# Strassen products over all row tiles, with 24 weight sums made early in the kernel

## The chip, the cores and the metric

The kernel runs on one core of one Trainium2 chip. The metric is the device time of one execution in microseconds (us), the median of several runs. One further execution was profiled; its trace is what is read below.

## What is computed

One layer of a hybrid decoder trunk, in float32, for 1024 tokens of width 2048. `h = RMSNorm(x)`; one input projection `proj = h @ w_in` gives queries, keys, values and gates of three head groups: dilated window attention (A), forgetting attention (B) and chunked gated linear attention (C, also GLA). Their outputs times SiLU(gate) are concatenated, projected and added to x:

```python
    proj = jnp.einsum('bsd,de->bse', h, w_in)
    ...
    mixed = jnp.concatenate([
        out_a.astype(h.dtype) * jax.nn.silu(az),
        out_b.astype(h.dtype) * jax.nn.silu(bz),
        out_c.astype(h.dtype) * jax.nn.silu(cz)], axis=-1)
    return x + jnp.einsum('bse,ed->bsd', mixed, w_out)
```

The change touches the last matrix product, `mixed @ w_out` (1024 x 2048 by 2048 x 2048), and work beside the first.

## The kernel before

Every float32 product is made of three rounded matmuls: an operand is split into a high and a low part (ScalarE rounds the high one, `hi`; VectorE subtracts, `lo`), and hi x hi, hi x lo and lo x hi are added up in PSUM. Each engine has its own program, written out in `build`; they meet at semaphores. SyncE (SP) only issues DMAs, in program order: where it waits, all that is queued behind it waits.

**Input projection.** It runs in column groups of 128 columns. A group has four quarters of the contraction (`kq`), each with one load of 256 KB into one of two buffers of `w_raw` (`load_quarter`), one rounding, one subtraction and 24 matmuls of 512 tokens (`half_quarter`). `load_quarter` waits until the quarter two places back is split. Groups 2 to 7 of the `C_ALONE` = 8 first groups have nothing else beside them; on SP they are a hardware loop of 24 loads (line 713). Behind that loop on SP stand the store `gate_stack <- gate_split` (line 767), then in `gla_loads(0)` the loads `rank_rows`, `gate_up`, `gate_bias` (734 to 736), which wait for that store to land, and only then the weights of group 8. GpSimd (POOL) makes `level_mask` (lines 1086 to 1105) when `gate_stack` has landed, and VectorE waits for it (`levels_ready`, line 1850) in front of group 8's second quarter.

**Attention.** One pair of heads after another, each beside four column groups. In the last pair (`LAST` = 9) there are no more input columns; TensorE then makes the first 512 output columns from 15 of the 16 row tiles of `mixed` (`early_quarter`), in three rounds, stored to `partial`. A row tile is 128 of the 2048 rows of the contraction. VectorE's order there is written in `last_body`: per slot the attention steps, the first weight split, the late steps, the other splits. Line 2045 is `scale`, the last step of a softmax; its result is turned by TensorE (line 2489).

**Output projection.** `out_quarter` makes columns 512 to 1023 from 16 row tiles into the 8 PSUM banks, one per 128 tokens. Then comes the Strassen part: columns 1024 to 2047 for 14 of the row tiles. Tokens, row tiles and columns are each cut into halves, which gives 2 x 2 blocks on each side and 7 products instead of 8. A product needs a sum or difference of two weight quarters (`FAST_WEIGHTS`) and of two row quarters (`FAST_ROW_SUMS`), both made by GpSimd (lines 1205 and 1217), and is then added by VectorE to one or two output blocks (`FAST_INTO`, `merge`, line 2222). A run of `FAST_RUNS` is a product (7 items, one per row tile, each 4 banks x 3 matmuls) or a "left" run: row tiles 8 and 9 for both column groups, and row tile 9 for columns 0 to 511, over all 8 banks:

```python
FAST_RUNS = [("product", 0), ("product", 1), ("left", 0), ("left", 1), ("left", 2)] + [("product", q) for q in range(2, 7)]
```

An item's weights go through one of four slots: two loads (`load_terms`), the sum on GpSimd (`weight_sum`), the split (`terms_hi`, `terms_lo`), three items ahead of TensorE (`fast_item`). At a run's first item TensorE waits until its banks' earlier tiles are merged (`out_summed`).

Of the kernel before, what the change touches and what calls it, by code (L numbers as in the profile page):

```python
# [4 lines left out]
P = 128  # L5
# [164 lines left out]
def weight_loads(n):  # L170

    r, j = run_of(n)
    kind, q = FAST_RUNS[r]
    if kind == "left":
        return [(LEFT_ROWS[q][j], LEFT_COLS[q])]
    one, op, two = FAST_WEIGHTS[q]
    return [(FAST_ROWS[kh][j], FAST_CGS[nh] * HALF) for kh, nh in ((one, two) if op is not None else (one,))]


def weight_op(n):  # L180

# [212 lines left out]
def build(nc, x, norm_g, w_in, a_q_gain, a_k_gain, b_q_gain, b_k_gain, fox_bias,  # L394
# [6 lines left out]
    mixed = nc.dram_tensor("mixed_scratch", (D_MODEL, SEQ), F32, kind="Internal").ap()  # L401
    partial = nc.dram_tensor("partial_scratch", (SEQ, HALF), F32, kind="Internal").ap()
# [3 lines left out]
    with ExitStack() as ctx:  # L406
# [60 lines left out]
        c_sum = sb("c_sum", [B_HEADS, SEQ], scope=first)  # L467
        gate_raw, gate_split = x_tile[0:GATE_ROWS, 0, 0:GATE_COLS], x_tile[0:GATE_ROWS, 1, 0:GATE_COLS]
# [83 lines left out]
        merged_into = [fast_out[0], fast_out[1], res]  # L552
# [96 lines left out]
        def _(sp):  # L649
# [312 lines left out]
            def load_fast_residual(c, t):  # L962
                cols = slice(FAST_CGS[c] * HALF, (FAST_CGS[c] + 1) * HALF)
                sp.dma_start(fast_out[c][:, t, :], x_rows[t * P:(t + 1) * P, cols]).then_inc(x_in[c], 16)

            def load_partial(t):
                sp.wait_ge(out_saved[t], 32)
                sp.dma_start(res[:, t, :], partial[t * P:(t + 1) * P, :]).then_inc(res_in[t], 16)

            def load_rows_again(th, kh, j):  # L970

                k = FAST_ROWS[kh][j]
                sp.wait_ge(quarter_done, 3 * (GROUPS + AHEAD) + EARLY - len(ROUNDS) + OUT_ORDER.index(k) + 1)
                sp.dma_start(raw_rows(th, kh, j), mixed[k * P:(k + 1) * P, th * HALF:(th + 1) * HALF])\
                    .then_inc(mix_in[0 if th == kh else 1 + kh], 16)

            def load_terms(n):
# [6 lines left out]
                for to, (k, col) in zip((t_ones[slot], t_twos[slot]), weight_loads(n)):  # L984
                    sp.dma_start(to, w_out_k[:, k, col:col + HALF]).then_inc(terms_in[slot], 16)
# [14 lines left out]
            for kk in range(3, 6):  # L1000
                load_out_quarter(1, kk)
            sp.wait_ge(mix_lo, MIX_ALL)
            load_res(1)
            for kk in range(6, KT):
# [5 lines left out]
                elif kk <= 11:  # L1010
# [3 lines left out]
                    else:  # L1014
                        for t in range(2 * (kk - 8), 2 * (kk - 8) + 2):
                            load_fast_residual(1, t)
                else:
                    load_rows_again(1, 1, kk - 12)
                    for t in range(2 * (kk - 12), 2 * (kk - 12) + 2):
                        load_fast_residual(0, t)  # L1020
            load_terms(2)
            load_rows_again(1, 1, 4)
            load_terms(3)
            load_rows_again(1, 1, 5)
            load_terms(4)
            load_terms(5)
            load_rows_again(1, 1, 6)
            load_terms(6)
            load_terms(7)
            for n in range(8, FAST_ITEMS):  # L1030
# [4 lines left out]
                if 8 <= n < 8 + FAST_K:  # L1035
                    load_rows_again(1, 0, n - 8)
                if 14 <= n < 18:
                    for t in range(2 * (n - 14), 2 * (n - 14) + 2):
                        load_partial(t)
                if 18 <= n < 18 + FAST_K:  # L1040
                    load_rows_again(0, 1, n - 18)
                if 28 <= n < 32:
                    for t in range(2 * (n - 28), 2 * (n - 28) + 2):
                        save_merged(2, t)
                if 45 <= n < 49:
                    save_merged(0, 4 + n - 45)
# [11 lines left out]
        def _(pool):  # L1058
# [20 lines left out]
            pool.memset(gate_raw, 0.0).then_inc(zeroed, 1)  # L1079

# [1573 lines left out]
```

## Time and profile before

| what | value |
|---|---|
| three runs | 2038.71 to 2040.92 us, median 2040.43 |
| the profiled execution | 2044.43 us |
| its span, first to last instruction | 2042.7 us, mean granted clock 0.998 |
| TensorE busy | 2008.2 us, 98% |
| VectorE busy | 1121.9 us, 55% |
| ScalarE busy | 891.1 us, 44% |
| GpSimd busy | 503.1 us, 25% |
| DMA | 223.20 MB, mean 109 GB/s |

Busy is time with an instruction under way; the rest is idle. A matmul of 512 columns is shown as 0.39 us long, but the next starts before it ends, so the pace is read from starts or from counts per stretch. An idle time is put down to the event that ended it. Idle time of an engine that is not the limit costs nothing by itself.

### The profile page before, as it was taken

Reading aid. Unit: us, or ns where it says so; the run is one execution under the profiler, and the core shown is the slowest. Engines: PE = TensorE matmul, PEld = TensorE weight load, DVE = VectorE, ACT = ScalarE, POOL = GpSimd, SP = SyncE. Lnnn points to the kernel's source line nnn. Section 1 sums busy time; section 2 is a strip of 40 time slices with the busy share of each in tenths; the row PEclk is TensorE's granted clock in tenths of the full one; section 3 lists DMA queues with packets and bytes.
Section 4 is the critical chain, followed back from the end, with each engine's and each line's share of the span. In section 5 each row is a group of like instructions: output and inputs, shape, how many; then the busy total and the mean of one; then the engine's idle time right before and its main releaser. Section 6 shows DMA issues by size and latency. Waiting matters only on the chain.

```text
span 2042.7 us, 28729 instructions
## 1 busy us (share of the span) xinstructions
PE 2008.2 (98%) x10024; PEld 1690.6 (83%) x10024; DVE 1121.9 (55%) x1733; ACT 891.1 (44%) x1504; POOL 503.1 (25%) x400
## 2 busy tenths in 40 slices
PE   6999999999999999999999999999999999999998
PEld 5788888888888888888888888888888887788787
DVE  7611456465445555555555555555555657613797
ACT  7311343444454445445454445445444556411242
POOL 0000343251531212222221212222122210002565
PEclk9999999999999999999999999999999999999999
DMA  7322424324332222222222222323232274466646
GB/s 236 81 72 71 116 68 109 100 82 103 94 98 78 61 85 78 87 67 72 87 72 85 64 89 79 107 58 98 83 97 71 85 249 145 134 200 222 237 155 196
DMA packets 204559, 223.20 MB, mean 109 GB/s; under 512 B 17336, under 2 KB 143336, under 8 KB 203328
## 3 DMA queue, kind: packets, MB, share of 16 engines
q1 hardware_dynamic: 187760, 191.73, 31.8%
q10 hardware_dynamic: 16720, 30.45, 4.0%
q8 instruction: 46, 0.75, 0.2%
q14 instruction: 33, 0.27, 0.0%
HBM read 173.35 MB, written 48.78 MB: 109 GB/s over the span
## 4 chain that ended last, share of the span: by engine, by line
PE 85%; DVE 7%; ACT 2%; DMA 2%; issue 2%; POOL 1%; SPq 0%; DVEq 0%; ACTq 0%; POOLq 0%
PE acc L2266 19%; PE acc L2268 19%; PE acc L2267 19%; PE pv L2504 4%; PE turned L2489 4%; PE scores L2481 2%; PE scores L2478 2%; DVE w_lo L1724 1%; DVE act_lo L2209 1%; DMA w_raw<-in_w_in_dram 1%; PE acc L2616 1%; DVE fast_out L2222 1%; PE acc L2553 1%; PE acc L2555 1%; PE acc L2554 1%
## 5 line engine op out<-in xcount | busy, mean ns | idle before, releaser
L2266 PE MATMUL acc<-act_hi,w_hi 128*128 128x512 f32 x1848 | 737.1, 399 | 2.5 <-DVE w_lo L1724 1.9
L2268 PE MATMUL acc<-act_hi,w_lo 128*128 128x512 f32 x1848 | 722.0, 391 | 0.0
L2267 PE MATMUL acc<-act_lo,w_hi 128*128 128x512 f32 x1848 | 720.7, 390 | 0.0
L2268 PEld LDWEIGHTS acc<-act_hi,w_lo 128*128 128x128 f32 x1848 | 346.9, 188 | 75.4
L2266 PEld LDWEIGHTS acc<-act_hi,w_hi 128*128 128x128 f32 x1848 | 347.5, 188 | 69.5 <-DVE w_lo L1724 4.8
L2267 PEld LDWEIGHTS acc<-act_lo,w_hi 128*128 128x128 f32 x1848 | 347.7, 188 | 65.2
L1724 DVE TENSOR_TENSOR w_lo<-w_raw,w_hi 128x512 fp32r<-128x512 f32 x223 | 199.4, 894 | 358.6 <-ACT w_hi L1239 358.3
L1545 ACT ACTIVATE prob<-prob,neg_max 128x128 f32<-128x128 f32 (+7 forms) x160 | 124.0, 775 | 251.1 <-DVE neg_max L2035 251.1
L1159 POOL TENSOR_TENSOR vz<-raw 32x512 f32<-32x512 f32 x72 | 85.6, 1189 | 468.3 <-ACT sq L1492 465.6
L1239 ACT ACTIVATE w_hi<-w_raw 128x512 fp32r<-128x512 f32 x223 | 139.1, 624 | 137.2 <-PE acc L2268 110.1
L2051 DVE TENSOR_TENSOR pt_lo<-turned,pt_hi 128x1024 fp32r<-128x1024 f32 (+1 forms) x120 | 114.9, 957 | 146.9 <-ACT pt_hi L1553 146.3
L1553 ACT ACTIVATE pt_hi<-turned 128x1024 fp32r<-128x1024 f32 (+1 forms) x120 | 97.6, 814 | 201.3 <-PE turned L2489 201.0
L1173 POOL TENSOR_TENSOR q_st<-raw,q_st 64x512 fp32r<-64x512 f32 x40 | 58.8, 1469 | 355.3 <-ACT q_st L1519 353.8
L2035 DVE CUSTOM_DVE_ANT_0 prob<-scores,logit_bias 128x128 f32<-128x128 f32 (+7 forms) x160 | 117.9, 753 | 40.3 <-PE scores L2481 39.6
L1282 ACT ACTIVATE stage<-acc 128x512 f32<-128x512 f32 x112 | 66.9, 597 | 113.0 <-PE acc L2268 112.7
L2489 PE MATMUL turned<-ident,prob 128*128 128x128 f32 x720 | 98.5, 273 | 1.9 <-DVE prob L2045 1.7
L2489 PEld LDWEIGHTS turned<-ident,prob 128*128 128x128 f32 x720 | 84.4, 141 | 13.0 <-issue 3.3
L2504 PE MATMUL pv<-pt_lo,v_st 128*128 128x256 f32 (+1 forms) x400 | 94.9, 292 | 0.0
L2504 PE MATMUL pv<-pt_hi,v_st 128*128 128x256 f32 (+1 forms) x400 | 88.3, 270 | 2.8 <-DVE pt_lo L2051 2.8
L2045 DVE TENSOR_SCALAR prob<-prob,inv_denom 128x128 f32<-128x128 f32 (+7 forms) x160 | 83.2, 520 | 5.7
L2504 PEld LDWEIGHTS pv<-pt_hi,v_st 128*128 128x128 f32 x400 | 75.9, 190 | 11.8 <-issue 3.5
L2481 PE MATMUL scores<-k_lo,q_st 128*128 128x128 f32 (+2 forms) x240 | 83.7, 353 | 0.0
(427 smaller groups left out, 3007.0 us busy)
## 6 DMA issues: line engine op xcount, KB each, us to landing
w_raw<-in_w_in_dram SPq DMA_DIRECT2D x240, 256.0 KB, 2.9
proj_scratch<-stage ACTq DMA_DIRECT2D x116, 256.0 KB, 2.1
w_raw<-in_w_out_dram SPq DMA_DIRECT2D x64, 256.0 KB, 3.5
raw<-proj_scratch SPq DMA_DIRECT2D x20, 512.0 KB, 3.4
logit_bias<-in_w_out_dram SPq DMA_DIRECT2D x35, 256.0 KB, 4.6
act_lo<-mixed_scratch SPq DMA_DIRECT2D x7, 1024.0 KB, 8.6
t_raw<-in_w_out_dram SPq DMA_DIRECT2D x28, 256.0 KB, 3.7
extra_raw<-in_w_out_dram SPq DMA_DIRECT2D x23, 256.0 KB, 3.5
```

Of the source, the lines that this page charges most:

```text
L1239: act.activation(w_hi[:, slot, :], w_raw[:, slot, :], ACT.Copy).then_inc(hi_done, 1)
L1545: act.activation(prob[:, j % 2, 0:n], prob[:, j % 2, 0:n], ACT.Exp, scale=-1.0, bias=neg_max[:, j:j + 1], accum_out=denom[:, j:j + 1]).the ...
L1553: act.activation(pt_hi[:, 0:n], turned[:, 0:n], ACT.Copy).then_inc(pth_done, 1)
L1724: dve.tensor_tensor(w_lo[:, slot, :], w_raw[:, slot, :], w_hi[:, slot, :].bitcast(F32), ALU.subtract)\
L2035: dve.tensor_tensor_reduce(out=prob[:, j % 2, 0:n], in0=scores[:, c0:c0 + n], in1=bias, scale=1.0, scalar=3e38, op0=ALU.add, op1=ALU.min, ...
L2051: dve.tensor_tensor(pt_lo[:, 0:n], turned[:, 0:n], pt_hi[:, 0:n].bitcast(F32), ALU.subtract)\
L2266: pe.matmul(acc, hi, xh, start=first, stop=False)
L2267: pe.matmul(acc, hi, xl, start=False, stop=False)
L2268: mm = pe.matmul(acc, lo, xh, start=False, stop=end)
L2481: mm = pe.matmul(scores[:, o + c0:o + c1], q, k_lo[:, h, c0:c1], start=False, stop=True)
L2489: mm = pe.transpose(turned[:, o:o + P], prob[:, q, c * P:(c + 1) * P], ident[:])
L2504: mm = pe.matmul(pv[:, (2 * (d % 2) + q) * P:(2 * (d % 2) + 2) * P], v_st[:, h, c, :], (pt_hi, pt_lo)[part][:, o:o + (2 - q) * P], start=( ...
```

## The change

- The Strassen part covers all 16 row tiles: 8 row tiles in each half, and row tile 9 stands last in the second half. Of the left runs only the one for columns 0 to 511 stays (one item), and it runs first. The products are renumbered.
- Products 2 and 6 (`FAST_ON_TOP`) start on the banks of products 0 and 4 without clearing them, so an output block gets the sum in one merge; product 0 and 4 then go into one block only.
- For products 1, 2 and 4 the 24 weight sums are made in groups 2 to 7 of the input projection: SP loads two weight quarters into `g_wide`, GpSimd adds them, SP stores the sum to `summed` in DRAM. In the Strassen part such an item has one load and no sum.
- Row tiles 8 and 9 of `mixed` are also stored to DRAM, since their halves are loaded again for row sums. The merges' targets and the loads of x and of `partial` into them trade places; a product's merges are spread over 6 items.
- In slot 28 of the last pair VectorE's late steps (the last `scale`) stand ahead of the slot's first split.

```diff
+LATE_FIRST = 28
...
 FAST_CGS = (2, 3)
-FAST_ROWS = (list(range(7)), [7] + list(range(LAST + 1, KT)))
-FAST_LEFT = (LAST - 1, LAST)
+FAST_ROWS = (list(range(LAST - 1)), [LAST - 1] + list(range(LAST + 1, KT)) + [LAST])
 FAST_K = len(FAST_ROWS[0])
-FAST_WEIGHTS = (((0, 1), ALU.subtract, (1, 1)), ((1, 0), ALU.subtract, (0, 0)), ((0, 0), ALU.add, (1, 1)),
-                ((0, 0), None, None), ((1, 1), None, None), ((0, 0), ALU.add, (0, 1)), ((1, 0), ALU.add, (1, 1)))
-FAST_ROW_SUMS = (None, None, ((0, 0), ALU.add, (1, 1)), ((1, 0), ALU.add, (1, 1)), ((0, 0), ALU.add, (0, 1)),
-                 ((1, 0), ALU.subtract, (0, 0)), ((0, 1), ALU.subtract, (1, 1)))
-FAST_INTO = (((1, 0, ALU.add), (1, 1, ALU.add)), ((0, 1, ALU.add), (0, 0, ALU.add)),
-             ((0, 0, ALU.add), (1, 1, ALU.add)), ((0, 1, ALU.add), (1, 1, ALU.subtract)),
-             ((1, 0, ALU.add), (0, 0, ALU.subtract)), ((1, 1, ALU.add),), ((0, 0, ALU.add),))
-FAST_RUNS = [("product", 0), ("product", 1), ("left", 0), ("left", 1), ("left", 2)] + [("product", q) for q in range(2, 7)]
-LEFT_ROWS = (FAST_LEFT, FAST_LEFT, FAST_LEFT[1:])
-LEFT_COLS = (FAST_CGS[0] * HALF, FAST_CGS[1] * HALF, 0)
+FAST_WEIGHTS = (((0, 1), ALU.subtract, (1, 1)), ((1, 0), ALU.subtract, (0, 0)), ((0, 0), ALU.add, (0, 1)),
+                ((0, 0), None, None), ((0, 0), ALU.add, (1, 1)), ((1, 1), None, None), ((1, 0), ALU.add, (1, 1)))
+FAST_ROW_SUMS = (None, None, ((1, 0), ALU.subtract, (0, 0)), ((1, 0), ALU.add, (1, 1)), ((0, 0), ALU.add, (1, 1)),
+                 ((0, 0), ALU.add, (0, 1)), ((0, 1), ALU.subtract, (1, 1)))
+FAST_ON_TOP = (2, 6)
+SUMMED_SOONER = (1, 2, 4)
+SOONER = [(q, j) for q in SUMMED_SOONER for j in range(FAST_K)]
+SOONER_AT = 0
+FAST_INTO = (((1, 0, ALU.add),), ((0, 1, ALU.add), (0, 0, ALU.add)), ((1, 1, ALU.add),),
+             ((0, 1, ALU.add), (1, 1, ALU.subtract)), ((1, 1, ALU.add),), ((1, 0, ALU.add), (0, 0, ALU.subtract)),
+             ((0, 0, ALU.add),))
+FAST_RUNS = [("left", 2)] + [("product", q) for q in range(7)]
+LEFT_ROWS = {2: (LAST,)}
+LEFT_COLS = {2: 0}
 RUN_SIZE = [FAST_K if kind == "product" else len(LEFT_ROWS[q]) for kind, q in FAST_RUNS]
 RUN_FIRST = [sum(RUN_SIZE[:r]) for r in range(len(FAST_RUNS))]
 RUN_LAST = [f + n - 1 for f, n in zip(RUN_FIRST, RUN_SIZE)]
 FAST_ITEMS = sum(RUN_SIZE)
 FAST_SLOTS = 4
+MERGE_STEPS = 6
 SPLIT_BEFORE = Q_OUT + EARLY + KT
 USED_BEFORE = 3 * (GROUPS + AHEAD) + EARLY - len(ROUNDS) + KT - 1
 FAST_SUMS = (len(FAST_INTO) - 2) * FAST_K
-ROW_SUM_STEP = [first + j for first in (9, 16, 23, 30, 37) for j in range(FAST_K)]
+ROW_SUM_STEP = [first + j for first in (4, 12, 20, 28, 36) for j in range(FAST_K)]
...
+    return weight_terms(q, j)[:1 if q in SUMMED_SOONER else 2]
+
+
+def weight_terms(q, j):
...
-            out += own[2 * (n - e - 1):2 * (n - e)]
+            out += [own[i] for i in range(len(own)) if e + 1 + i * MERGE_STEPS // len(own) == n]
...
+        sooner = [[g_wide[:, (2 * i + e) * HALF:(2 * i + e + 1) * HALF] for e in range(2)] for i in range(2)]
...
-            with sp.Fori(AHEAD, C_ALONE) as s:
-                for kq in range(4):
-                    load_quarter(s, kq, COL_CQ + s * P)
+            def load_sooner(i):
+
+                if i == 0:
+                    sp.wait_ge(x_turned, 4 * NT)
+                elif i >= 2:
+                    sp.wait_ge(small_saved, 16 * i)
+                for to, (k, col) in zip(sooner[i % 2], weight_terms(*SOONER[i])):
+                    sp.dma_start(to, w_out_k[:, k, col:col + HALF]).then_inc(row_summed, 16)
+
+            def store_sooner(i):
+                sp.wait_ge(t_summed, i + 1)
+                sp.dma_start(summed[i * P:(i + 1) * P, :], sooner[i % 2][0]).then_inc(small_saved, 16)
+
+            for n in range(4 * (C_ALONE - AHEAD)):
+                load_quarter(AHEAD + n // 4, n % 4, COL_CQ + (AHEAD + n // 4) * P)
+                if 0 <= n - SOONER_AT - 1 < len(SOONER):
+                    store_sooner(n - SOONER_AT - 1)
+                if 0 <= n - SOONER_AT < len(SOONER):
+                    load_sooner(n - SOONER_AT)
+            for i in range(4 * (C_ALONE - AHEAD) - SOONER_AT - 1, len(SOONER)):
+                store_sooner(i)
+            sp.wait_ge(small_saved, 16 * (len(SOONER) + 1))
...
+                if n == 7:
+                    store_pair(LAST - 1)
                 if n == 10:
                     sp.wait_ge(mix_lo, mixed_by(KK_GATED, 1))
+                    sp.wait_ge(mixed_saved, 16 * LAST)
...
+                kind, q = FAST_RUNS[run_of(n)[0]]
+                if kind == "product" and q in SUMMED_SOONER:
+                    i = SOONER.index((q, run_of(n)[1]))
+                    sp.dma_start(t_ones[slot], summed[i * P:(i + 1) * P, :]).then_inc(terms_in[slot], 16)
+                else:
+                    for to, (k, col) in zip((t_ones[slot], t_twos[slot]), weight_loads(n)):
+                        sp.dma_start(to, w_out_k[:, k, col:col + HALF]).then_inc(terms_in[slot], 16)
...
+            sp.wait_ge(o_done, LAST + 3)
+            sp.dma_start(mixed[LAST * P:(LAST + 1) * P, :], vz[:]).then_inc(mixed_saved, 16)
             sp.wait_ge(mix_lo, MIX_ALL)
+            sp.wait_ge(mixed_saved, 16 * PAIRS)
...
+            for i, (q, _j) in enumerate(SOONER):
+                pool.wait_ge(row_summed, 32 * (i + 1))
+                pool.tensor_tensor(sooner[i % 2][0], sooner[i % 2][0], sooner[i % 2][1], FAST_WEIGHTS[q][1]).then_inc(t_summed, 1)
...
                     steps(slot)
+                    if slot == LATE_FIRST:
+                        late(slot)
                     for n in early_at(slot)[:1]:
                         split_next(n + EARLY_AHEAD)
-                    late(slot)
+                    if slot != LATE_FIRST:
+                        late(slot)
                     for n in early_at(slot)[1:]:
...
+                on_top = kind == "product" and q in FAST_ON_TOP
...
-                    pe.matmul(banks[b], hi, t_his[slot], start=first, stop=False)
-                    pe.matmul(banks[b], hi, t_los[slot], start=False, stop=False)
-                    mm = pe.matmul(banks[b], lo, t_his[slot], start=False, stop=at_end)
+                    pe.matmul(banks[b], hi, t_his[slot], start=first and not on_top, stop=False,
+                              skip_group_check=on_top)
+                    pe.matmul(banks[b], hi, t_los[slot], start=False, stop=False, skip_group_check=on_top)
+                    mm = pe.matmul(banks[b], lo, t_his[slot], start=False, stop=at_end, skip_group_check=on_top)
```

SP's queue in the input projection. Before, each pass of the loop of line 713 issues four loads, and this stands behind it:

```order
L656 ISA [waits lo_done]
L656 DMA w_raw<-in_w_in_dram 128x4x128
L713 COMPARE_AND_BRANCH
L767 DMA gate_scratch<-x_tile 80x1408 [waits gate_lows]
L734 DMA rank_rows<-gate_scratch 80x1024 [waits gate_saved,c_saved,c_done]
L735 DMA gate_up<-gate_scratch 80x96
L736 DMA gate_bias<-in_gla_gate_bias_dram 96x1
L656 DMA w_raw<-in_w_in_dram 128x4x128 [waits lo_done] x2
```

Now the loop is written out; these are its last pass and what follows (`t_summed` is GpSimd's sum, `small_saved` counts landed stores):

```order
L668 DMA w_raw<-in_w_in_dram 128x4x128 [waits lo_done]
L736 DMA summed_scratch<-g_wide 128x512 [waits t_summed]
L732 DMA g_wide<-in_w_out_dram 128x512 [waits small_saved]
L732 DMA g_wide<-in_w_out_dram 128x512
L736 DMA summed_scratch<-g_wide 128x512 [waits t_summed]
L798 DMA gate_scratch<-x_tile 80x1408 [waits gate_lows,small_saved]
```

Between two weight loads of the input projection there are now a wait for a sum, a store and two loads, and `gate_scratch` stands behind the last sum and the landing of its store.

GpSimd's queue from `iota` to the masks, now:

```order
L1127 IOTA dist_i 128x1024 [waits consts]
L1131 MEMSET x_tile 80x1408 [waits x_turned]
L1135 TENSOR_TENSOR g_wide<-g_wide 128x512 [waits row_summed] x24
L1142 MEMSET level_mask 128x896 [waits gate_lows,c_saved,gate_saved,small_saved,c_done]
L1143 MEMSET ident_both 128x256
```

The 24 sums of line 1135 are new; the other rows stood in the same order without them.

VectorE's queue at the last scale of the last pair, before:

```order
L2035 ISA neg_max 128x1
L2155 TENSOR_TENSOR act_lo<-w_raw,act_hi 128x512
L2043 RECIPROCAL inv_denom<-denom 128x1
L2045 TENSOR_SCALAR prob<-prob,inv_denom 128x1024
L2155 TENSOR_TENSOR w_lo<-extra_raw,w_hi 128x512
```

and now:

```order
L2094 ISA neg_max 128x1
L2102 RECIPROCAL inv_denom<-denom 128x1
L2104 TENSOR_SCALAR prob<-prob,inv_denom 128x1024
L2217 TENSOR_TENSOR act_lo<-w_raw,act_hi 128x512
L2217 TENSOR_TENSOR w_lo<-extra_raw,w_hi 128x512
```

The reciprocal and the scale have moved ahead of one weight split.

## Rows read from the trace of the kernel before

**Rows 1.** The page: busy engines, and the chain that ended last.
```profile
PE 2008.2 (98%) x10024; PEld 1690.6 (83%) x10024; DVE 1121.9 (55%) x1733; ACT 891.1 (44%) x1504; POOL 503.1 (25%) x400
...
PE 85%; DVE 7%; ACT 2%; DMA 2%; issue 2%; POOL 1%; SPq 0%; DVEq 0%; ACTq 0%; POOLq 0%
```
**Rows 2.** Windows: stretch, length, busy us (and instructions) of each engine, clock, DMA share, GB/s.
```profile
1850.00:1900.00 50.00, 50.00 (x221) 41.16 (x220) 19.31 (x28) 9.89 (x16) 14.87 (x12) 1.00 0.78 265
80.00:220.00 140.00, 139.66 (x616) 115.31 (x616) 25.22 (x33) 29.14 (x44) 7.79 (x21) 1.00 0.32 86
1950.00:2000.00 50.00, 50.00 (x220) 40.97 (x219) 49.52 (x53) 22.09 (x38) 36.71 (x24) 1.00 0.49 164
```
**Rows 3.** Timeline (start, length) and waits (us, times, longest) in the Strassen part.
```profile
1921.78 0.39 PE L2618 MATMUL side<-w_hi,act_lo 128*128 128x512 f32 x1
1923.03 0.47 PE L2616 MATMUL acc<-t_hi,act_hi 128*128 128x512 f32 x1 [0.86 <-DVE fast_out L2222]
...
2037.09 0.69 DVE L2222 TENSOR_TENSOR fast_out<-fast_out,scores 128x512 f32<-128x512 f32 x1
...
PE acc L2616 <- DVE fast_out L2222: 1.7, 2, 0.9
PE acc L2616 <- DVE w_lo L2201: 0.3, 1, 0.3
```
**Rows 4.** Timeline at the last scale of the last pair.
```profile
1771.82 0.39 PE L2555 MATMUL acc<-act_hi,act_lo 128*128 128x512 f32 x1
1773.66 0.52 PE L2489 MATMUL turned<-ident,prob 128*128 128x128 f32 x3 [1.46 <-DVE prob L2045]
...
1771.23 0.18 ACT L1545 ACTIVATION_READ_ACCUMULATOR prob<-prob,neg_max 128x1 f32 x1
...
1772.77 0.75 DVE L2045 TENSOR_SCALAR prob<-prob,inv_denom 128x1024 f32<-128x1024 f32 x1
```
**Rows 5.** Timeline of SyncE's queue, at the loop's first load and behind the loop.
```profile
88.78 0.39 SPq L656 DMA_DIRECT2D w_raw<-in_w_in_dram  x1
...
208.10 0.36 SPq L767 DMA_DIRECT2D gate_scratch<-x_tile  x1
212.00 0.34 SPq L734 DMA_DIRECT2D rank_rows<-gate_scratch  x1
...
213.33 3.79 SPq L656 DMA_DIRECT2D w_raw<-in_w_in_dram  x2
```
**Rows 6.** Timeline of GpSimd behind the loop; in brackets the idle time before.
```profile
212.06 0.85 POOL L1086 MEMSET level_mask<- 128x896 f32 x1 [152.50 <-DMA gate_scratch<-x_tile]
...
218.62 4.80 POOL L1105 TENSOR_SCALAR_AFFINE_SELECT level_mask<-level_mask 128x64 f32<-128x64 f32 x14
```
**Rows 7.** Timeline of ScalarE where TensorE ends group 7.
```profile
226.22 0.60 ACT L1282 ACTIVATE stage<-acc 128x512 f32<-128x512 f32 x1 [2.04 <-PE acc L2268]
```
**Rows 8.** Landings (KB, us) of late loads: alone at 1944.98, followed at 1919.49, four at 1825.
```profile
logit_bias<-in_w_out_dram SPq DMA_DIRECT2D x1, 256.0 KB, 3.3
...
1948.39 1.45 POOL L1205 TENSOR_TENSOR t_raw<-t_raw,logit_bias 128x512 f32<-128x512 f32 x1 [1.45 <-DMA logit_bias<-in_w_out_dram]
...
logit_bias<-in_w_out_dram SPq DMA_DIRECT2D x1, 256.0 KB, 3.8
...
fast_out<-in_x_dram SPq DMA_DIRECT2D x2, 256.0 KB, 4.4
```
**Rows 9.** Landings in the stretch 80 to 220 us.
```profile
w_raw<-in_w_in_dram SPq DMA_DIRECT2D x29, 256.0 KB, 2.9
proj_scratch<-stage ACTq DMA_DIRECT2D x12, 256.0 KB, 2.1
```
**Rows 10.** GpSimd's weight sums and row sums: ns least/median/most, first and last start.
```profile
L1205 POOL TENSOR_TENSOR t_raw<-t_raw,logit_bias x20: 1285/1296/1835, 1812.2 to 2026.5; 128x512 f32<-128x512 f32 x20
...
L1217 POOL TENSOR_TENSOR row_sum<-act_lo,act_hi x21: 1281/1687/1837, 1919.8 to 2011.8; 128x512 f32<-128x512 f32 x21
```
**Rows 11.** Windows of TensorE alone, behind a wait of 2.8 us that ended at 1688.79.
```profile
1688.00:1692.00 4.00, 3.21 (x14) 0.57 0.81 229
```

More of the change, by code:

```diff
@@ L182, in weight_op @@
     kind, q = FAST_RUNS[run_of(n)[0]]
-    return FAST_WEIGHTS[q][1] if kind == "product" else None
+    return FAST_WEIGHTS[q][1] if kind == "product" and q not in SUMMED_SOONER else None
 def weights_landed(n):
@@ L401, in build @@
     mixed = nc.dram_tensor("mixed_scratch", (D_MODEL, SEQ), F32, kind="Internal").ap()
+    summed = nc.dram_tensor("summed_scratch", (len(SOONER) * P, HALF), F32, kind="Internal").ap()
     partial = nc.dram_tensor("partial_scratch", (SEQ, HALF), F32, kind="Internal").ap()
@@ L983, in load_terms @@
                     sp.wait_ge(lo_done, SPLIT_BEFORE - 3 + n)
-                for to, (k, col) in zip((t_ones[slot], t_twos[slot]), weight_loads(n)):
-                    sp.dma_start(to, w_out_k[:, k, col:col + HALF]).then_inc(terms_in[slot], 16)
+                kind, q = FAST_RUNS[run_of(n)[0]]
+                if kind == "product" and q in SUMMED_SOONER:
+                    i = SOONER.index((q, run_of(n)[1]))
+                    sp.dma_start(t_ones[slot], summed[i * P:(i + 1) * P, :]).then_inc(terms_in[slot], 16)
+                else:
+                    for to, (k, col) in zip((t_ones[slot], t_twos[slot]), weight_loads(n)):
+                        sp.dma_start(to, w_out_k[:, k, col:col + HALF]).then_inc(terms_in[slot], 16)
             def save_merged(c, t):
@@ L1015, in _ @@
                         for t in range(2 * (kk - 8), 2 * (kk - 8) + 2):
-                            load_fast_residual(1, t)
+                            load_fast_residual(t)
                 else:
-                    load_rows_again(1, 1, kk - 12)
+                    if kk == 12:
+                        load_rows_again(0, 0, FAST_K - 1)
+                    load_rows_again(1, 0, kk - 12)
                     for t in range(2 * (kk - 12), 2 * (kk - 12) + 2):
-                        load_fast_residual(0, t)
+                        load_partial(t)
             load_terms(2)
-            load_rows_again(1, 1, 4)
+            load_rows_again(1, 0, 4)
             load_terms(3)
-            load_rows_again(1, 1, 5)
+            load_rows_again(1, 0, 5)
             load_terms(4)
             load_terms(5)
-            load_rows_again(1, 1, 6)
+            load_rows_again(1, 0, 6)
             load_terms(6)
             load_terms(7)
+            load_rows_again(1, 0, 7)
             for n in range(8, FAST_ITEMS):
@@ L1035, in _ @@
                 if 8 <= n < 8 + FAST_K:
-                    load_rows_again(1, 0, n - 8)
+                    load_rows_again(1, 1, n - 8)
                 if 14 <= n < 18:
                     for t in range(2 * (n - 14), 2 * (n - 14) + 2):
-                        load_partial(t)
+                        load_first_residual(t)
                 if 18 <= n < 18 + FAST_K:
                     load_rows_again(0, 1, n - 18)
-                if 28 <= n < 32:
-                    for t in range(2 * (n - 28), 2 * (n - 28) + 2):
+                if 20 <= n < 24:
+                    for t in range(2 * (n - 20), 2 * (n - 20) + 2):
                         save_merged(2, t)
-                if 45 <= n < 49:
-                    save_merged(0, 4 + n - 45)
+                if 48 <= n < 52:
+                    save_merged(0, 4 + n - 48)
             for t in range(4):
@@ L1211, in sum_rows @@
                 if u == 0:
-                    pool.wait_ge(mix_in[0], mix_landed(0) + 16 * 2 * FAST_K)
-                elif j == 0 and q in (3, 4):
-                    pool.wait_ge(mix_in[q - 2], mix_landed(q - 2) + 16 * FAST_K)
+                    pool.wait_ge(mix_in[0], mix_landed(0) + 16 * FAST_K)
+                    pool.wait_ge(mix_in[1], mix_landed(1) + 16 * FAST_K)
+                elif j == 0 and q == 3:
+                    pool.wait_ge(mix_in[2], mix_landed(2) + 16 * FAST_K)
+                elif j == 0 and q == 5:
+                    pool.wait_ge(mix_in[3], mix_landed(3) + 16 * FAST_K)
                 if u >= 4:
@@ L2213, in merge @@
                 r, b, c, t, op = MERGES[i]
-                if c == 2:
+                if merged_before(i) is None and c == 0:
                     dve.wait_ge(res_in[t], 48)
                 elif merged_before(i) is None:
-                    dve.wait_ge(x_in[c], 16 * (NT // X_BUFS + NT))
+                    dve.wait_ge(x_in[c % 2], 16 * (NT // X_BUFS + NT))
                 if merged_before(i) is not None:
```

23 lines of the change are left out of this document (14 added, 9 removed).

## The prediction

> **What bounds the kernel now.** I read the page first. TensorE is busy for 2008.2 us, 98% of the span, and the chain of waits that ended last lies on it for 85% [rows 1], so a change counts only where it adds or removes matmuls or idle time of TensorE. A full stretch holds 221 matmuls of 512 columns in 50 us [rows 2], 0.227 us each; a quarter of a column group (24 of them) takes 5.44 us.
>
> Then the list of TensorE's waits, and the places near the change. In the Strassen part matmuls start 0.23 us apart but for three places: two where banks wait for VectorE's merges (1921.78 to 1923.03 us is one, the other is like it), and one where a split is late [rows 3]. Ahead of it the last scale of the last pair holds the turn behind it back to 1773.66 us, where the matmul before had started at 1771.82; a split stands in front of that scale on VectorE [rows 4].
>
> Last I read the stretch into which the 24 sums go. TensorE idles for 0.3 of 140 us there [rows 2]; SyncE has one 256 KB weight load per quarter, 24 of them from 88.78 us on [rows 5], and GpSimd is empty for 152 us [rows 6]. That looks like free room. What the reader should see is the chain behind the loop: SyncE sends gate_scratch at 208.10, rank_rows at 212.00, the next weight load at 213.33 [rows 5]; that load lands 2.9 us later [rows 9], at 216.2, and TensorE ends the loop's last group at 226.22, when ScalarE takes the bank [rows 7]. With 1.5 us for both splits the chain has 8.5 us to spare and no more.
>
> **The change, part by part.**
>
> *Matmuls.* Before: 7 products x 7 row tiles x 4 banks x 3 = 588, left rows 5 x 8 x 3 = 120, in sum 708. After: 7 x 8 x 4 x 3 = 672 and 24, in sum 696. 12 fewer x 0.227 = **-2.7 us**, on the path.
>
> *Waits for merges.* The 16 merges of left rows that TensorE ran into are gone, and products 2 and 6 add onto the banks of 0 and 4, so merges fall from 72 to 48 on a VectorE that is busy 49.5 of 50 us there [rows 2]. The three gaps hold 1.02 + 1.06 + 0.43 us above the normal spacing (the waits view counts 1.7 and 0.3 of it as idle), and the next matmuls start 0.1 us late each time, together 0.3: **-2.8 us** [rows 3], with 0 as the other bound. The new first run has one item; its 8 merges stand behind the residual adds. The last residual add ends some 1.0 us after the column group before, then come a split (0.7) and four merges at 0.69 [rows 3], 4.5 us in all, while TensorE spends 5.44 us on the left item before it needs those banks: nothing.
>
> *Weight sums.* GpSimd's late sums fall from 35 to 16, and 24 weight pairs become one load each. TensorE waited for none of them (the late split at 2018 is counted), so I cost this at zero; what hid them is the three items of lead. Row sums rise from 35 to 40, splits from 54 to 57: inside the same cover.
>
> *Rows LAST-1 and LAST to DRAM.* Two stores, each waited for behind others on SyncE. A 256 KB store lands in 2.1 us [rows 9], 512 KB in perhaps 3; the next weight load then has a quarter of 5.44 us in hand. Zero; uncovered it would be up to 3 us.
>
> *The last scale.* ScalarE has the sum of its exponentials at 1771.23 + 0.18 = 1771.41 us; the reciprocal and the scale can then end near 1772.5 and not at 1773.52 [rows 4]. **-1.0 us** (between 0, if the split behind it turns late, and 1.6, the whole gap).
>
> Savings: 2.7 + 2.8 + 1.0 = **6.5 us**.
>
> *The early sums.* Per sum SyncE waits for the last one, stores it (0.4 us of its queue), issues two loads (0.37 us for the first), the second lands after L, GpSimd starts 0.11 us later (1948.39 against a landing at 1948.28, [rows 8]), adds for 1.30 us [rows 10], SyncE wakes about 0.1 us later. Two buffers are declared, but the load of sum i is queued behind the wait for sum i-1, so nothing overlaps: a cycle is 2.3 + L. L isn't in this stretch of the trace; the nearest rows are the same kind of pair late in the kernel: 3.3 us with nothing near it, 3.8 with one more load close behind, and in a burst of four the last two take 4.4 at the median [rows 8]. Here a store goes ahead and a weight load follows 0.5 us later, between the second and third case: **L = 3.9, cycle 6.2 us**, bounds 3.3 and 4.6 (a little above that last row). That is more than the 5.44 us of a quarter, so SyncE falls behind from the first quarters on.
>
> From 88.78 + 0.4: the 24th sum is ready for its store at 89.2 + 24 x 6.2 - 0.4 = 237.6 us. SyncE then waits for that store to land (2.2), sends gate_scratch and waits for it (3.9), sends rank_rows, gate_up, gate_bias (1.33), then the first weight load of the next group, which needs 2.9 to land [rows 9] and 1.5 for both splits: 249.4 us, against 226.2 at which TensorE wants it. **+23.2 us**, part of it as waits inside the loop once a load is late by more than the 10 us that two buffers give.
>
> GpSimd now makes level_mask behind the sums, 11.4 us from gate_scratch's landing [rows 6], and VectorE waits for it in front of a split: 0.5 us more, and 0.7 for the gate arithmetic behind it. **+1.2 us**. A long gap also costs clock: after the 2.8 us wait that ended at 1688.79 the granted clock was 0.57 at the mean of 4 us [rows 11], so it stood at 0.5, the lower of TensorE's two levels (1.2 GHz), for some 3.4 of them. Half of that is lost, once: **+1.7 us**.
>
> Here a rule speaks against the change. The rows show the pair's 3.9 us entirely in the open. The Trainium skill (DMA: Bandwidth & Descriptors, section Rules for kernel authors) says to issue a DMA early, compute, and wait on its semaphore late, since the fixed setup cost then overlaps. With loads two sums ahead, the roughly 2 us of fixed cost it gives would leave a cycle of some 4.2 us, an estimate from that page, and no delay.
>
> **Sum.** 23.2 + 1.2 + 1.7 - 6.5 = **+19.6 us**. The profiled execution took 2044.4 us, 4.0 above the median of the three runs; I add the difference to the median: 2040.4 + 19.6 = **2060 us**.
>
> **Rivals.**
>
> 1. *The sums stay hidden (faster).* The transfer engines are only 32% busy in this stretch [rows 2], so pairs might land sooner than late in the kernel. L counts 24 times: 24 x (3.9 - L) must reach 23.2 us, so the case decides at L = 2.9. Then 2040.4 - 6.5 = 2034 us. For it: a single weight load takes 2.9 here [rows 9]. Against it: the best second load on record is 3.3, and that alone still leaves +8.8. By the bandwidth and fixed latency that the Trainium skill gives (the same page, sections Bandwidth and Latency and other measured facts) a pair would land after some 3.5 us, L = 3.1, and the time would be about 2039 us, an estimate from that page. Chance 0.12.
>
> 2. *The best pair is the rule.* L = 3.3, cycle 5.6: 14.4 us less; without the small extras +8.8 - 6.5 = +2.3, 2043 us. Chance 0.10.
>
> 3. *GpSimd's sum is slowed.* Row sums on GpSimd take 1.69 us at the median where VectorE works beside them, weight sums 1.30 [rows 10]. Against it: VectorE is busy for 25 of 140 us here [rows 2], so most sums would meet nothing. 24 x 0.39 = 9.4 us more: 2069 us. The Trainium skill (GPSIMD Engine Reference, section Specifications) says that GpSimd contends with VectorE instructions that have two SBUF inputs, which the splits are. Chance 0.13.
>
> 4. *Crowded transfers.* L = 4.6: 16.8 us more, 2077 us. Chance 0.10.
>
> 5. *The Strassen part gives less.* VectorE stays near its limit, new first waits appear and 2.8 us don't come back: 2063 us. Chance 0.10. That the early sums relieve nothing late is already in my zero.
>
> My own case keeps 0.45.
>
> **The numbers.** Likeliest 2060 us. The range reaches from 2040 (cases 2 and the slow end of 1) to 2076, leaving out nearly all of case 1 and the top of case 4. A measurement of this kernel tells 0.2%, 4 us, from no change. Faster by more: 0.12. Within: 0.10 (case 2). Slower: 0.78.
>
> **What would show it.** SyncE's stores to summed_scratch stand 6.2 us apart, not 5.44; gate_scratch leaves near 240 us, not 208; TensorE is idle for over 10 us in sum ahead of the first head's group, with weight splits waiting for DMA; after it a stretch at clock 0.5. In the Strassen part no gap over 0.5 us, and its 696 matmuls take 158 us where 708 and the gaps took 163. It is wrong if the stores are 5.4 us apart, or if the gap ahead of the first head is under 3 us.

## The result, and the profile after

The changed kernel takes **2072.62 us** (median, 2071.05 to 2075.17) against 2040.43 before: ratio 1.0161, 95% interval 1.015 to 1.0172, 32 us slower. Forecast were 2060 us, range 2040 to 2076. The profiled execution took 2072.30 us, its span is 2070.2 us at a mean granted clock of 0.994.

The page of the kernel after, lines that answer to [rows 1] and two groups of its DMA issues (KB each, median us to landing):

```profile
PE 2014.0 (97%) x10012; PEld 1690.1 (82%) x10012; DVE 1085.6 (52%) x1717; ACT 893.4 (43%) x1512; POOL 503.1 (24%) x410
...
PE 79%; DMA 7%; DVE 6%; POOL 2%; ACT 2%; issue 2%; SPq 2%; DVEq 0%; ACTq 0%; POOLq 0%
...
g_wide<-in_w_out_dram SPq DMA_DIRECT2D x48, 256.0 KB, 4.2
...
summed_scratch<-g_wide SPq DMA_DIRECT2D x24, 256.0 KB, 2.0
```

TensorE has 12 matmuls fewer, as counted, and the chain of waits now lies on it for 79%, where it was 85%: the loads into `g_wide` have taken 5% of it and GpSimd's sums 2%. Windows of the kernel after, which answer to [rows 2]:

```profile
80.00:220.00 140.00, 127.94 (x528) 101.09 (x527) 23.53 (x29) 24.68 (x38) 24.88 (x19) 0.96 0.62 173
1980.00:2030.00 50.00, 50.00 (x220) 40.98 (x219) 31.86 (x51) 20.76 (x36) 22.01 (x17) 1.00 0.34 106
```

TensorE's waits in 80 to 270 us (us in total, times, longest):

```profile
PE acc L2328 <- DVE w_lo L1783: 28.0, 16, 11.4
```

TensorE, idle for only 0.3 of 140 us here before [rows 2], waits 28 us for weight splits, 11.4 of them at once. The other part of what it loses here it loses by its clock: the granted clock has a mean of 0.96 in 80 to 220 us, where it was 1.00. The queue of SyncE shows why it waits. All 24 stores of sums as one group (first and last start):

```profile
L736 SPq DMA_DIRECT2D summed_scratch<-g_wide x24: 326/326/327, 95.5 to 252.0; - x24
```

The timeline: one link of the chain, with GpSimd's sum in it, then the tail behind the loop, which answers to [rows 5], and TensorE's restart:

```profile
204.16 0.33 SPq L736 DMA_DIRECT2D summed_scratch<-g_wide  x1
204.53 0.93 SPq L732 DMA_DIRECT2D g_wide<-in_w_out_dram  x2
205.50 0.43 SPq L668 DMA_DIRECT2D w_raw<-in_w_in_dram  x1
211.04 0.33 SPq L736 DMA_DIRECT2D summed_scratch<-g_wide  x1
...
209.72 1.29 POOL L1135 TENSOR_TENSOR g_wide<-g_wide 128x512 f32<-128x512 f32 x1 [5.58 <-DMA g_wide<-in_w_out_dram]
...
254.07 0.34 SPq L798 DMA_DIRECT2D gate_scratch<-x_tile  x1
257.32 0.33 SPq L765 DMA_DIRECT2D rank_rows<-gate_scratch  x1
...
258.63 0.98 SPq L668 DMA_DIRECT2D w_raw<-in_w_in_dram  x2
...
263.59 0.77 PE L2328 MATMUL acc<-act_hi,w_hi 128*128 128x512 f32 x1 [11.36 <-DVE w_lo L1783]
```

(252.0 - 95.5) / 23 = 6.80 us from store to store, where a quarter's matmuls take 5.44 us. The link shown is 6.88 us long; single ones lie between 6.3 and 7.8. SyncE sends nothing in it from 206.0 to 211.0 us: it waits for a sum whose loads have not landed, and the next weight load stands behind that wait.

Where the whole difference lies follows from two groups that both kernels have: the rows of head pairs leaving PSUM (`o_full`, first and last start), and the first bank of the Strassen part. Before:

```profile
L1564 ACT ACTIVATE o_full<-pv x40: 589/593/597, 629.0 to 1784.3; 64x512 f32<-64x512 f32 x40
...
L2616 PE MATMUL acc<-t_hi,act_hi x34: 394/394/473, 1872.6 to 2035.4; 128*128 128x512 f32 x34
```

After:

```profile
L1623 ACT ACTIVATE o_full<-pv x40: 588/592/597, 667.1 to 1818.3; 64x512 f32<-64x512 f32 x40
...
L2679 PE MATMUL acc<-t_hi,act_hi x34: 394/394/398, 1906.5 to 2064.0; 128*128 128x512 f32 x34
```

By the first head pair 38.1 us are lost. The Strassen part then takes 157.5 us instead of 162.8, 5.3 us back, and the last scale about one more: 38.1 - 5.3 - 1 = 31.8, close to the 32.2 by which the medians differ. (What follows these last matmuls is another 1.1 us shorter in the two traces, 6.2 against 7.3 us, so the account is good to a microsecond or two.) The two profiled executions differ by only 27.9 us, because the one before had an accident of its own, told under the unexpected.

### The profile page after: what moved, and what is told of

Same layout as the page of the kernel before. It is cut to its first block, busy times and chain, and to the rows that moved or that the text cites. A ratio compares the mean times of both kernels' runs of the same rounds, so it can differ in the third digit from the quotient of the medians.

```text
span 2070.2 us, 28678 instructions
## 1 busy us (share of the span) xinstructions
PE 2014.0 (97%) x10012; PEld 1690.1 (82%) x10012; DVE 1085.6 (52%) x1717; ACT 893.4 (43%) x1512; POOL 503.1 (24%) x410
## 4 chain that ended last, share of the span: by engine, by line
PE 79%; DMA 7%; DVE 6%; POOL 2%; ACT 2%; issue 2%; SPq 2%; DVEq 0%; ACTq 0%; POOLq 0%
PE acc L2328 16%; PE acc L2330 16%; PE acc L2329 16%; DMA g_wide<-in_w_out_dram 5%; PE pv L2566 4%; PE turned L2551 4%; PE scores L2543 2%; PE scores L2540 2%; POOL g_wide L1135 2%; DVE w_lo L1783 1%; DMA w_raw<-in_w_in_dram 1%; PE acc L2679 1%; PE acc L2682 1%; PE acc L2681 1%; PE scores L2679 1%
```

## The experiments

The theory after the result, A: the loss is a serial chain in SyncE's queue (wait for the sum, store, two loads, landing, sum) of 6.8 us a link against 5.44 us, and the tail behind it; all other parts gain about 6 us. A kernel named e1, e2 and so on is the changed kernel with the edit shown, unless said otherwise. Where a ratio is given, it is to the kernel before, with its 95% interval.

**e1: no sum made early.**

```diff
-SUMMED_SOONER = (1, 2, 4)
+SUMMED_SOONER = ()
```

> The changed kernel with no weight sum made early: all 40 are made by GpSimd in the Strassen part, from two loads each. Theory A (a serial chain of sum, store, load and landing in SP's queue, 6.8 us a link against 5.44 us of matmuls a quarter, and the tail behind it, are the whole loss): the first head's group starts near 229 us again instead of 264, and the rest keeps its gains, so 2034 us (2031 to 2037). Rival B (the gains of the Strassen part come from the early sums): GpSimd or the second loads hold that part up, gaps come back in it, 2038 to 2045 us.

Measured 2043.39 us, ratio to before 1.0015 (1.0005 to 1.0024). Theory A is right on the front: the first `o_full` starts at 629.7 us. But the rest of the change without the early sums is 3 us *slower* than before: that is rival B, which had gaps come back in the Strassen part. Windows 1925 to 2000 us of e1, of e4 (below) and of e8 (below):

```profile
1925.00:2000.00 75.00, 69.33 (x286) 52.22 (x285) 74.58 (x69) 31.87 (x52) 65.64 (x41) 1.00 0.52 167
```
```profile
1925.00:2000.00 75.00, 75.00 (x329) 61.43 (x328) 48.68 (x76) 31.03 (x54) 32.68 (x26) 1.00 0.40 121
```
```profile
1925.00:2000.00 75.00, 75.00 (x329) 61.43 (x328) 51.81 (x75) 30.11 (x52) 30.16 (x23) 1.00 0.55 176
```

In e1 VectorE is busy 74.58 of 75 us with 69 instructions, 1.08 us each; in e4 it needs 48.68 us for 76, 0.64 each. Its timeline in e1 beside GpSimd's points to the cause:

```profile
1938.81 1.18 DVE L2263 TENSOR_TENSOR w_lo<-w_raw,w_hi 128x512 fp32r<-128x512 f32 x1
1939.91 1.77 DVE L2271 TENSOR_TENSOR act_lo<-row_sum,act_hi 128x512 fp32r<-128x512 f32 x1
1941.61 0.68 DVE L2284 TENSOR_TENSOR res<-res,turned 128x512 f32<-128x512 f32 x1
...
1939.40 1.73 POOL L1261 TENSOR_TENSOR w_raw<-w_raw,logit_bias 128x512 f32<-128x512 f32 x1
1941.10 1.74 POOL L1276 TENSOR_TENSOR row_sum<-act_lo,act_hi 128x512 f32<-128x512 f32 x1
```

GpSimd runs without a pause there, 1.7 us a sum. VectorE's subtractions with both inputs in SBUF take up to 1.8 us instead of 0.68; the merge (`res<-res,turned`), which reads one input from PSUM, keeps its 0.68. The split of row sums is the clearest case (ns least/median/most, first and last start), in the kernel before, in the kernel after and in e1:

```profile
L2209 DVE TENSOR_TENSOR act_lo<-row_sum,act_hi x35: 674/1776/1794, 1905.2 to 2019.2; 128x512 fp32r<-128x512 f32 x35
```
```profile
L2271 DVE TENSOR_TENSOR act_lo<-row_sum,act_hi x40: 676/684/686, 1928.1 to 2034.6; 128x512 fp32r<-128x512 f32 x40
```
```profile
L2271 DVE TENSOR_TENSOR act_lo<-row_sum,act_hi x40: 675/1772/1783, 1895.0 to 2013.1; 128x512 fp32r<-128x512 f32 x40
```

The kernel before had the long splits too, so this cost was already in its trace. The Trainium skill (GPSIMD Engine Reference, section Specifications) says that GpSimd shares its SBUF interface with VectorE and contends with VectorE instructions that have two SBUF inputs; these rows agree, on both sides of the pair.

**e2: 16 early sums.** `SUMMED_SOONER = (1, 2)`.

> The changed kernel with 16 early sums (products 1 and 2) instead of 24. Theory A: 15 links at 6.8 us instead of 5.44 us lose 20.5 us, of which the two buffers of w_raw take up about 6 (as with 24 sums: 23 links lose 31.5 us and TensorE was late by 25.6 us at the end of the loop); TensorE regains nothing, as it is the bound, but the tail behind the loop is gone, since the last sum is out before the loop ends: 2034 + 15 = 2049 us (2045 to 2053). Rival C (each early sum costs a fixed share of the whole loss, whatever its order): 2034 + 38 x 2/3 = 2059 us.

Measured 2050.92 us, ratio 1.0045 (1.0028 to 1.0062): near theory A (2049), not at a fixed price per sum (2059). The Strassen part takes 157.4 us (1885.7 to 2043.1). TensorE's waits in 80 to 270 us are 9.9 us, the longest 2.7, so there is no tail:

```profile
PE acc L2328 <- DVE w_lo L1783: 9.9, 8, 2.7
```

**e3: gate_scratch is stored in the loop.** All 24 sums as in the change.

```diff
+                if n == 3:
+                    sp.wait_ge(gate_lows, 2)
+                    sp.dma_start(gate_stack[:, :], gate_split).then_inc(gate_saved, 16)
...
-            sp.wait_ge(gate_lows, 2)
-            sp.dma_start(gate_stack[:, :], gate_split).then_inc(gate_saved, 16)
```

> The changed kernel with the store to gate_scratch issued in the loop, behind the fourth quarter, instead of behind the wait for the last sum's store; all 24 early sums stay. Theory A: in the tail the 3.3 us from the store to the loads that wait for it go (254.07 to 257.32 us), for rank_rows and for GpSimd's level_mask: 2069.4 us (2068 to 2071). Rival D (level_mask alone or the weight quarters set the start of the first head): less than 1 us, 2072 us.

Measured 2072.00 us: 0.6 less than the change, which is no difference by the ranges of the two, and not 3.2. The tail does shrink by 3.3 us, as expected: from the last store to TensorE's restart it takes 8.3 us (252.87 to 261.17) instead of 11.55. But the last store is 0.8 us later, with the store to `gate_scratch` now in the loop. So TensorE restarts 2.4 us sooner, and the granted clock comes back where it came back without the edit. TensorE alone in the kernel after, then in e3:

```profile
258.00:260.00 2.00, 0.00 (x0) 0.50 0.72 178
264.00:266.00 2.00, 2.00 (x6) 0.50 0.70 262
266.00:268.00 2.00, 2.00 (x8) 0.67 0.15 44
268.00:270.00 2.00, 2.00 (x10) 1.00 1.03 299
```
```profile
258.00:260.00 2.00, 0.00 (x0) 0.50 0.85 247
264.00:266.00 2.00, 2.00 (x7) 0.50 0.25 76
266.00:268.00 2.00, 2.00 (x8) 0.75 1.09 298
268.00:270.00 2.00, 2.00 (x11) 1.00 1.13 257
```

The 2.4 us won are worked off at 0.5, 1.2 GHz, so they are worth some 1.2, an estimate from these windows; the first matmul with rank_rows is 1.7 us sooner (266.4 against 268.1) and the first `o_full` 0.4. Where the rest went isn't settled.

**e4: the sums pipelined.** Same loads, sums and stores as in the change; four pairs of buffers (two in `g_wide`, one each in `count` and `term`, free by then), loads issued two sums ahead, 24 sums spread over 20 quarters, gate_scratch stored as in e3.

```diff
+                elif i >= 4:
+                    sp.wait_ge(small_saved, 16 * (i - 2))
...
+                for i in range(len(SOONER)):
+                    if SOONER_AT + i * SOONER_OVER // len(SOONER) == n:
+                        if i >= 2:
+                            store_sooner(i - 2)
+                        load_sooner(i)
```

> 24 early sums that truly overlap: four pairs of buffers instead of two, SP issues the loads of a sum two sums ahead of its store, the 24 sums are spread over 20 of the 24 quarters, and the store to gate_scratch is issued in the loop. The same loads, sums and stores. Theory A: no link of SP waits for a landing, the loop runs at TensorE's pace again: 2034 us (2032 to 2038), first head's group near 229 us. Rival E (the transfers themselves, 18.9 MB more in 130 us, slow the weight quarters or GpSimd's port slows VectorE): the loop stays late by 10 us or more, 2045 to 2062 us.

Measured **2035.16 us**, ratio 0.9971 (0.996 to 0.9983); run again as e11, 2035.47, ratio 0.998 (0.997 to 0.999). The first head's rank_rows matmul is back at 230.2 us. Its window 80 to 220 us:

```profile
80.00:220.00 140.00, 138.48 (x609) 113.95 (x609) 29.63 (x33) 29.11 (x44) 44.80 (x56) 1.00 0.73 220
```

Its landings in 95 to 210 us (KB each, median us):

```profile
w_raw<-in_w_in_dram SPq DMA_DIRECT2D x22, 256.0 KB, 4.4
g_wide<-in_w_out_dram SPq DMA_DIRECT2D x20, 256.0 KB, 4.8
summed_scratch<-g_wide SPq DMA_DIRECT2D x12, 256.0 KB, 3.4
```

The transfers are more crowded than in the change (0.73 against 0.62 of the engines, 220 against 173 GB/s), and the loads into `g_wide` and the stores land later (4.8 against 4.2, 3.4 against 2.0), yet TensorE idles for 1.5 of 140 us. So the same transfers cost almost nothing once nobody waits for them in the open. The run changes four things together: the number of buffers, the lead of the loads, their spread and the place of the gate_scratch store. Only the last was tried alone (e3), and it gave almost nothing. That is the sentence of the Trainium skill which the prediction weighed against the change (DMA: Bandwidth & Descriptors, Rules for kernel authors), and e4 bears it out.

**e5: the pair of loads ahead of the weight quarter** in each round.

```diff
-                load_quarter(AHEAD + n // 4, n % 4, COL_CQ + (AHEAD + n // 4) * P)
                 if 0 <= n - SOONER_AT - 1 < len(SOONER):
...
+                load_quarter(AHEAD + n // 4, n % 4, COL_CQ + (AHEAD + n // 4) * P)
```

> The changed kernel (24 early sums, two pairs of buffers), but in each round of the loop SP issues the pair of loads for the next sum ahead of the weight quarter instead of behind it. Theory A1 (the landing took 4.5 us instead of 3.9 because the pair stands behind the weight load): the pair lands 0.5 us or more sooner, stores to summed_scratch stand 6.3 us apart instead of 6.81, TensorE's waits in the loop shrink by some 11 us: 2061 us (2058 to 2064). Rival A2 (the pair's landing is set by its own bytes): stores 6.8 us apart, 2072 us.

Measured 2071.71 us, and the group of stores shows them (250.6 - 93.8) / 23 = 6.82 us apart. A1 fell: the order in the queue isn't what makes the landing long. Its trace also warns of idle time as a measure: in 80 to 264 us TensorE is busy for 160.12 us at a mean clock of 0.94, in the change for 155.61 at 0.95, and its waits for splits are 23.5 us instead of 28.0. The time is the same, because SyncE's chain sets the pace: what TensorE doesn't idle, it spends on more stretches at the lower clock.

```profile
L736 SPq DMA_DIRECT2D summed_scratch<-g_wide x24: 321/326/327, 93.8 to 250.6; - x24
```

**e6: one load per early sum.** GpSimd adds the first term to itself.

```diff
-                for to, (k, col) in zip(sooner[i % 2], weight_terms(*SOONER[i])):
+                for to, (k, col) in zip(sooner[i % 2][:1], weight_terms(*SOONER[i])):
...
-                pool.wait_ge(row_summed, 32 * (i + 1))
+                pool.wait_ge(row_summed, 16 * (i + 1))
```

> The changed kernel with one load per early sum instead of two: the second term of the 24 early sums is left out (GpSimd adds the first to itself). The chain stays: wait, store, load, landing, sum. If only the issue of the second load (0.5 us) goes: stores 6.3 us apart, 2061 us. If the bytes in flight set the landing too (a single load of this size lands in 2.9 us beside an idle queue, and the pair in 4.5): 1.6 us less, stores 5.4 to 5.5 us apart, that is the pace of the weight quarters, and of the 38 us before the first head only the tail is left: 2040 to 2046 us.

Measured 2039.50 us. The stores stand (218.1 - 93.9) / 23 = 5.40 us apart, the pace of the quarters, and a load lands in 3.8 us at the median; the group of stores, then the landings in 95 to 218 us:

```profile
L736 SPq DMA_DIRECT2D summed_scratch<-g_wide x24: 326/326/344, 93.9 to 218.1; - x24
```
```profile
g_wide<-in_w_out_dram SPq DMA_DIRECT2D x22, 256.0 KB, 3.8
```

A link is 1.4 us shorter. In the change the first load of a pair lands in 4.0 us at the median, and the second, issued some 0.5 us later, in 4.4 (mean 4.6). So the single load is hardly faster than the first of two; most is won because nobody waits for the second any more, 4.9 us behind the first issue at the median. The sum itself is shorter too with the same operand twice (1.14 us mean, not 1.30). The stores now keep the pace of the quarters, 5.44 us, and 33 us lie between this kernel and the change. What is left is a wait of 2.9 us behind the loop, and about 4 us against e4.

**e7: the kernel before with the last scale in front of the splits.**

```diff
+                    if slot == LATE_FIRST:
+                        late(slot)
                     for n in early_at(slot)[:1]:
                         split_next(n + EARLY_AHEAD)
-                    late(slot)
+                    if slot != LATE_FIRST:
+                        late(slot)
```

> The kernel before with the last scale in front of the weight splits and nothing else. By the step of the prediction: 1.0 us less, 2039.3 us (2038.9 to 2040.0), the wait for prob 0.5 us instead of 1.5. Rival: the split behind it is late by as much, 2040.3 us.

Measured 2039.02 us, ratio 0.9992 (0.9983 to 1.0001): 1.4 us less by the medians, no difference by the interval. In its trace TensorE's waits for prob from 1600 us on are 0.6 us in sum, the longest 0.4. The trace shows the wait gone; the size fits the step, but the timing can't prove it.

**e8: e1 without the 40 late weight sums** (left out of the computation; both loads of each pair stay).

```diff
 def weight_op(n):
...
-    return FAST_WEIGHTS[q][1] if kind == "product" and q not in SUMMED_SOONER else None
+    return None
```

> The kernel with no early sums (e1), and GpSimd's 40 late weight sums left out of the computation; both loads of every pair and the 40 row sums stay. Theory G (GpSimd and VectorE slow each other: in e1 a row split on VectorE took 1.77 us instead of 0.68 and a row sum on GpSimd 1.7 instead of 1.3, and VectorE was busy for all of 1960 to 2000 us): the gaps of the Strassen part go, it takes 157.5 us as with early sums, 2034 us (2032 to 2036). Rival H (the second loads and their landings hold that part up): gaps stay, 2040 to 2043 us.

Measured 2033.42 us: theory G. With all second loads in place, but GpSimd busy 30.16 instead of 65.64 of 75 us, TensorE has no gap (third window under e1). It isn't the loads that hold up the Strassen part. In e1 TensorE waits there for VectorE's splits of weights, 5.7 us in sum; in e8 no wait is left.

**e9 and e10: e4 with 16 sums (`(1, 2)`) and 8 (`(2,)`).**

> The pipelined kernel (e4) with 16 early sums (products 1 and 2) instead of 24. With serial early sums (e2) 16 were enough to leave no gap in the Strassen part (157.4 us), so that part stays at 157.5 us; in the loop a third of the added transfers goes, and of the 1.1 us by which the first head starts later than before some 0.4 or more: 2034.6 us (2033.6 to 2035.3), against 2035.2 for 24. Rival: product 4's weight sums beside the row sums cost waits, 2036 us or more.

> The same with 8 early sums (product 2). GpSimd then has 32 weight sums beside 40 row sums in the Strassen part. By theory G (GpSimd and VectorE slow each other while both are full) gaps come back where products 1 and 4 sum weights and rows at once, some 2 of e1's 5.7 us less front cost: 2036 us (2034.5 to 2038). If the two engines keep the lead of four items there: 2034 us.

> The pipelined kernel with 24 early sums again, beside the two above on one chip: 2035.2 us (2034.5 to 2036), 0.25% below the kernel before.

On one chip, against 2039.68 before: 16 sums 2035.63 us (0.9981, 0.9972 to 0.999), 8 sums 2037.73 (0.9986, 0.9977 to 0.9995), 24 sums 2035.47. 16 early sums gain nothing over 24, and with 8, slower by 2 us, the waits for splits in the Strassen part are back (1.5 us in the trace). e9 came out a little above its range; its trace has one wait of 2.3 us at the loop's start, ending at 103.53 us, and the clock falls behind it (windows of TensorE alone):

```profile
100.00:104.00 4.00, 1.75 (x8) 1.00 0.21 79
104.00:108.00 4.00, 4.00 (x13) 0.58 0.84 246
```

**e12: e4 with the sums begun three quarters later.** `SOONER_AT = 3`, `SOONER_OVER = 18`.

> The pipelined kernel with 24 early sums that begin three quarters later (behind the gate arithmetic) and are spread over 18 quarters. In e4 and e11 the whole front cost was one wait of 1.0 to 1.2 us at 102 us, where the first two pairs of loads, the weight quarter and VectorE's gate arithmetic meet. If that meeting is the cause, the wait goes, the first head starts at 228.9 us instead of 230.2, and the median is 2034.2 us (2033.3 to 2035.0). If the wait only moves to another place, 2035.4 us.

Measured **2034.27 us** (2033.19 to 2034.86), ratio 0.9968 (0.9956 to 0.998): the lowest median of the kernels that compute the whole layer. From e4 (0.996 to 0.9983) the ratios don't tell it apart. The wait at 102 us is gone; the first rank_rows matmul starts at 229.7 us, nearly a microsecond later than forecast.

## Why the prediction was right, and where it wasn't

The time fell inside the range, and the chief mechanism was the one forecast; but the term for the chain was 14 us too small, and the term for the Strassen part came out by luck.

- *Matmuls, -2.7.* 10024 became 10012 [rows 1 against the page after].
- *Merges and late split, -2.8.* The size came, but the reason was at best a part of it. The Strassen part shrank by 5.3 us as forecast, but e1 has the same 48 merges and only the one left run and takes 167.4 us (1873.4 to 2040.8), 4.6 more than before, with 80 sums on GpSimd where there were 70. Fewer merges alone don't close the gaps: they go where GpSimd's weight sums are gone too (e4, e8). Whether fewer sums would do with the 72 merges of before, no run shows.
- *Weight sums off the late path, 0.* **This step failed.** "TensorE waited for none of them" was true of waits by name; but these sums stretch VectorE's subtractions, and TensorE waits for those. The rows were there: VectorE busy 49.52 of 50 us [rows 2], row sums at 1.69 us instead of 1.30 [rows 10]. Early sums, pipelined, are worth 8.2 us (e1 against e4); the rest of the change alone costs 3. In the sum the two errors cancelled, which was luck.
- *Last scale, -1.0.* Consistent with e7, not shown by its time.
- *Rows 8 and 9 to DRAM, 0.* No wait for them shows in the trace after.
- *The chain, cycle 2.3 + L with L = 3.9.* Mechanism right, **L mis-sized**: 6.80 - 2.3 = 4.5 us, near the upper bound of 4.6, and between the median (4.4) and the mean (4.6) of the second loads in the trace. 23 x 0.6 = 14 us, which is the whole distance, 14.2, from the predicted restart at 249.4 us to 263.59. Of the near rows [rows 8] the burst of four (4.4 us) came nearest: a store, a pair and a weight load follow each other here, 173 GB/s on average.
- *Tail.* From the last store to TensorE's restart 11.8 us forecast, 11.55 measured (252.04 to 263.59).
- *level_mask +1.2, clock +1.7.* VectorE waited 5.0 us for level_mask, and TensorE worked 3.7 us at half clock, 1.9 lost. From the restart (+37.4) to the first `o_full` (+38.1) only 0.7 of the 2.9 is left. The forecast took the clock to fall once; it fell in the loop as well (mean 0.96 in 80 to 220 us), but there SyncE's chain sets the pace, and e5, with more of it, took the same time.
- *Sum.* 14 - 2 = +12 us over the forecast of +19.6 makes +32. Rival 4 (L = 4.6) had the mechanism; its 2077 us overshoots, as L was a little smaller and the extras of the restart mostly vanished. Rival 3 lay as near with its 2069 us but fell, as early sums took 1.29 us at the median; rival 1's 2034 us is what the overlap built in e4 gives (2035).

## What to carry to other kernels

Buffers overlap nothing by being two: look in the issuing queue for the wait that stands between them, and compare the length of a link with the pace of the work beside it, since a link inside that pace costs little (e6) and each microsecond above it counts once per link. A sum moved off GpSimd can pay through VectorE, though nobody waits for the sum: read the durations of VectorE's instructions with two SBUF inputs while GpSimd is busy. A microsecond taken off a long wait can be worth half or less while the clock is still down (e3: 2.4 us of wait, 0.4 at the first `o_full`).

## What was unexpected in the hardware

- GpSimd and VectorE slow each other: 1.7 us a sum instead of 1.29, up to 1.77 us a subtraction instead of 0.68, merges from PSUM unchanged at 0.68 (e1).
- A short wait can cost more than its length, but doesn't always. The profiled execution before waited 2.8 us for pt_lo until 1688.79 us and then ran at clock 0.57 for 4 us [rows 11]; in e1 the same wait was 2.8 us, with a clock of 0.50 in 1689 to 1693 us and 0.70 in the 4 us after. In the twelve other profiles of this study it was between 0.7 and 1.7 us, and the clock stayed at 1.00 in the 4 us around its end. The longer wait and the lower clock cost the one before some 3 us and e1 some 5 (its profiled execution took 2048.77 us, the median is 2043.39), and that is why the profiled executions differ by less than the medians. The length of the wait doesn't decide it alone: in the kernel after, waits of 2.65, 2.41 and 2.12 us (to 151.59, 178.75 and 205.55 us) had a stretch at 0.5 behind them, but one of 2.33 us (to 233.97) had none, nor had one of 2.92 us in e6 (to 229.57).
- Landings grew beside the new traffic: 256 KB of w_raw in 2.9 us before [rows 9] and 4.8 in the loop after (95 to 250 us); ScalarE's stores of 256 KB 2.1 and 4.9 us, in another queue. But the rate alone doesn't order them: at 220 GB/s in e4 w_raw lands in 4.4 us. Why the second load of a pair needs 4.4 us here and 3.3 or 3.8 late in the kernel [rows 8] isn't settled; it isn't the order in the queue (e5).
